# Residual rows ahead of the next stage, no GpSimd drain at two Blocks' ends, and turns between half products in a two-layer hybrid trunk

## What is computed

```python
def odd_mixer(xn, w_in, conv_w, conv_b, w_out):
    gate_b, gate_c, h = jnp.split(xn @ w_in, 3, axis=-1)
    u = gate_c * h
    y = causal_depthwise_conv(u, conv_w) + conv_b
    return (gate_b * y) @ w_out

def expert_block(args):
    xb, e = args
    return (jax.nn.silu(xb @ w_gate[e]) * (xb @ w_up[e])) @ w_down[e]
...
    h = h + mixer(rms_norm(h, mix_norm_g[layer]), ...)
    h = h + hierarchical_moe(rms_norm(h, ffn_norm_g[layer]), ...)
```

## Time and profile before

| | |
|---|---|
| median of 3 runs | 2219.44 us (2216.64 to 2220.0) |
| the profiled execution's own time | 2220.42 us |
| its span in the trace | 2218.7 us |
| PE busy | 1897.2 us (86%) |
| DVE busy | 1228.1 us (55%) |
| ACT busy | 853.2 us (38%) |
| POOL busy | 311.2 us (14%) |
| mean granted clock of TensorE | 0.887 of full speed |

### The profile page before, as it was taken

How to read it: one execution, slowest core, us unless ns; L and a number is a source line. 1 busy time by engine, 2 the same in 40 slices (tenths; PEclk the granted TensorE clock), 3 DMA queues, 4 the chain that set the end, 5 groups by cost and what they waited for, 6 DMA issues and landing times. The chain is left out here.

```text
span 2218.7 us, 25775 instructions
## 1 busy us (share of the span) xinstructions
PE 1897.2 (86%) x9607; PEld 1569.5 (71%) x9608; DVE 1228.1 (55%) x1570; ACT 853.2 (38%) x912; POOL 311.2 (14%) x230
## 2 busy tenths in 40 slices
PE   8999977977589999986999991799999948999970
PEld 7888866767467777874888771588887847888760
DVE  5222115545564553566999883533224557999863
ACT  4110003311223333234888872211112126888850
POOL 0000003000100000112444320000000112443310
PEclk9999985655789999997999995799999978999995
DMA  6321134230200002446999965521124348999927
GB/s 214 129 89 68 48 127 153 71 67 7 77 1 1 1 1 94 162 158 255 363 376 375 374 239 200 180 57 38 47 66 160 133 175 313 383 385 375 364 117 303
DMA packets 146455, 374.22 MB, mean 169 GB/s; under 512 B 40174, under 2 KB 75246, under 8 KB 121614
## 3 DMA queue, kind: packets, MB, share of 16 engines
q1 hardware_dynamic: 117462, 320.82, 39.1%
q0 software_dynamic: 19680, 34.22, 4.1%
q10 hardware_dynamic: 9216, 17.93, 2.1%
HBM read 331.34 MB, written 75.10 MB: 183 GB/s over the span
## 5 line engine op out<-in xcount | busy, mean ns | idle before, releaser
L1037 PE MATMUL ex_ps_h<-even_split 128*128 128x512 f32 x768 | 194.9, 404 | 9.7 <-DVE even_split L1151 9.4
L1037 PE MATMUL ex_ps_h<-odd_split 128*128 128x512 f32 x768 | 195.0, 404 | 7.8 <-DVE odd_split L1151 7.6
L1037 PEld LDWEIGHTS ex_ps_h<-even_split 128*128 128x128 f32 x768 | 141.8, 191 | 49.0 <-DVE even_split L1151 15.2
L1037 PEld LDWEIGHTS ex_ps_h<-odd_split 128*128 128x128 f32 x768 | 141.7, 191 | 47.1 <-DVE odd_split L1151 14.2
L364 PE MATMUL in_ps<-in_w_hi,in_xT_hi 128*128 128x512 f32 (+1 forms) x448 | 169.6, 378 | 1.7 <-DVE in_xT_lo L311 1.7
L364 PE MATMUL in_ps<-in_w_lo,in_xT_hi 128*128 128x512 f32 (+1 forms) x448 | 168.9, 377 | 0.0
L364 PE MATMUL in_ps<-in_w_hi,in_xT_lo 128*128 128x512 f32 (+1 forms) x448 | 168.9, 377 | 0.0
L1418 PE MATMUL conv_ps<-conv_xT_hi,conv_w_hi 128*128 128x512 f32 x384 | 152.0, 396 | 7.5 <-DVE conv_xT_lo L1352 6.6
L1418 PE MATMUL conv_ps<-conv_xT_lo,conv_w_hi 128*128 128x512 f32 x384 | 151.3, 394 | 0.0
L1418 PE MATMUL conv_ps<-conv_xT_hi,conv_w_lo 128*128 128x512 f32 x384 | 151.2, 394 | 0.0
L319 DVE COPY in_stage<-in_ps 128x512 f32<-128x512 f32 (+1 forms) x56 | 36.7, 656 | 197.9 <-PE in_ps L364 197.9
(11 more groups left out here) (329 smaller groups left out, 4175.2 us busy)
## 6 DMA issues: line engine op xcount, KB each, us to landing
all_region<-in_moe_w_gate SPq DMA_DIRECT2D x16, 1024.0 KB, 9.6
all_region<-in_moe_w_up SPq DMA_DIRECT2D x16, 1024.0 KB, 17.8
all_region<-in_moe_w_down SPq DMA_DIRECT2D x16, 1024.0 KB, 16.3
experts_w_gu<-in_moe_w_gate SPq DMA_DIRECT2D x16, 1024.0 KB, 9.9
experts_w_gu<-in_moe_w_up SPq DMA_DIRECT2D x16, 1024.0 KB, 20.2
experts_w_d<-in_moe_w_down SPq DMA_DIRECT2D x16, 1024.0 KB, 15.3
all_region<-in_ev_w_in SPq DMA_DIRECT2D x12, 1024.0 KB, 8.5
proj<-in_stage ACTq DMA_DIRECT2D x48, 256.0 KB, 2.0
```

What stands on the lines that cost most here:

```text
L1037: last = pe.matmul(ps_h[:, u % 2, :], a[:, u % 2, k, :], w[:, k, :], start=(k == 0 and j == 0), stop=(k == KT - 1 and j == 2))
```

## The change

It has three parts.

1. A class `NextRows` holds a view of `region` as 8 tiles and 8 semaphores. SP loads the residual stream's 8 x tiles into it at the end of `experts`, after DVE has reported (`finished`) that it is done. `mix_and_conv` and `finish` use these tiles and load only the ya tiles themselves. In `mix_and_conv` the normed rows and the first column block's raw weights move to the place of `zT_hi`, the raw weights' loads move behind the first four tiles' ya loads, and SP waits for all stores and all norms before it loads column block 1. In `finish` the ya tiles get 8 places, so no load waits for a sum.
2. The Blocks of `project_and_route` and `experts` are opened with `no_gpsimd_drain=True`: POOL executes no DRAIN at their ends. The text calls this "the drain goes"; it holds for four ends, two in each layer.
3. In `mix_and_conv` PE's order changes: five turns come first instead of four, and each of the three others stands between halves (12 matmuls) of the products, where before two of them stood between whole products (24 matmuls) and the last two together behind the third.

Core of the diff:

```diff
@@ -130,8 +130,8 @@
                 self.all[:, gate:gate + qkv].rearrange("p (u n) -> p u n", u=2),
                 self.all[:, gate + qkv:gate + qkv + nq].rearrange("p (u n) -> p u n", u=2))
-    def normed_rows(self):
-        return self.all[:, 0:2 * D].rearrange("p (u n) -> p u n", u=2)
+    def stream_rows(self):
+        return self.all[:].rearrange("p (t n) -> p t n", t=NT)
     def gate_up(self):
         return self.all[:, 0:2 * KT * DE].rearrange("p (j k n) -> p j k n", j=2, k=KT)
@@ -516,7 +516,8 @@
             m.sem(n) for n in ("eps_ready", "bf_ready", "filled", "cleared", "coded", "listed"))
         shifted, exps = m.sem("shifted"), m.sem("exps")
-        with nc.Block() as block:
+
+        with nc.Block(no_gpsimd_drain=True) as block:
             @block.sync
             def _(sp):
                 if rows is not None:
@@ -869,7 +870,18 @@
                 last.then_inc(counted, 1)
-def experts(nc, name, data, lists, slots, most, ident):
+class NextRows:
+
+
+    def __init__(self, m, name, src, region):
+        self.src, self.rows, self.loaded = src, region.stream_rows(), m.sems(name, NT)
+
+    def load(self, sp):
+        for t in range(NT):
+            sp.dma_start(self.rows[:, t, :], self.src[t * P:(t + 1) * P, :]).then_inc(self.loaded[t], 16)
+
+
+def experts(nc, name, data, lists, slots, most, ident, following):
@@ -899,6 +911,7 @@
         FIRST, SECOND, DOWN = range(3)
+        done, finished = m.sb("done", [P, 1]), m.sem("finished")
         zeroed, x_turned = m.sem("zeroed"), m.sems("x_turned", B)
         gathered, idx = lists.gathered, lists.idx
         scattered = m.sems("scattered", U)
@@ -971,6 +985,9 @@
                     with sp.Fori(0, STEPS) as i:
                         round_(w, i)
                 waves(sp, wave, first=1)
+
+                sp.wait_ge(finished, 1)
+                following.load(sp)
             @block.gpsimd
             def _(pool):
@@ -1186,6 +1203,8 @@
                     low(*this, DOWN)
                 dve.memset(data.later_rows, 0.0).then_inc(zeroed, 1)
                 rounds(dve, start, step, lambda last: hidden(*last))
+                dve.drain()
+                dve.memset(done[:], 0.0).then_inc(finished, 1)
 def constants(nc, cst, block):
...
@@ -1214,8 +1233,11 @@
     YA = 4
     with Pool_(nc, name) as m:
         raw = region.conv_weights()
-        xn = region.normed_rows()
-        xin = z_places[0][:].rearrange("p k n -> p (k n)").rearrange("p (t n) -> p t n", t=NT)
+        xin, x_loaded = ahead_rows.rows, ahead_rows.loaded
+        place = z_places[0][:].rearrange("p k n -> p (k n)")
+        xn = place[:, 0:2 * D].rearrange("p (u n) -> p u n", u=2)
+
+        raw_0 = place[:, 2 * D:2 * D + 3 * KT * P].rearrange("p (j k n) -> p j k n", j=3, k=KT)
         ya = z_places[1][:].rearrange("p k n -> p (k n)").rearrange("p (u c n) -> p u c n", u=YA, c=2)
         xT_hi, xT_lo = m.sb("xT_hi", [P, KT, S], F32R), m.sb("xT_lo", [P, KT, S], F32R)
         w_hi = m.sb("w_hi", [P, 3, KT, P], F32R)
...
@@ -1245,7 +1267,6 @@
             @block.sync
             def _(sp):
                 def load_rows(t):
-                    sp.dma_start(xin[:, t, :], src[t * P:(t + 1) * P, :]).then_inc(x_loaded[t], 16)
                     for c in range(2):
                         at = c * S + t * P
                         sp.dma_start(ya[:, t % YA, c, :], slots[at:at + P, :]).then_inc(ya_loaded[t % YA], 16)
@@ -1254,12 +1275,12 @@
                     sp.wait_ge(mixed, t + 1)
                     sp.dma_start(mix_out[t * P:(t + 1) * P, :], xin[:, t, :]).then_inc(stored, 16)
-                for t in range(YA):
+                load_rows(0)
+                sp.dma_start(gains[:], row_of(gain)).then_inc(gain_loaded, 16)
+                for t in range(1, YA):
                     load_rows(t)
-                    if t == 0:
-                        sp.dma_start(gains[:], row_of(gain)).then_inc(gain_loaded, 16)
-                    if t < 3:
-                        sp.dma_start(raw[:, t, :, :], w_k[:, :, PARTS[t] * D:PARTS[t] * D + P]).then_inc(raw_loaded[t], 16)
+                for j in range(3):
+                    sp.dma_start(raw_0[:, j, :, :], w_k[:, :, PARTS[j] * D:PARTS[j] * D + P]).then_inc(raw_loaded[j], 16)
                 for t in range(YA, NT):
                     sp.wait_ge(mixed, t - YA + 1)
@@ -1271,6 +1292,9 @@
                                  allow_slow_non_contiguous=True).then_inc(taps_loaded, 16)
                 for t in range(NT):
                     store_rows(t)
+
+                sp.wait_ge(stored, 16 * NT)
+                sp.wait_ge(normed, NT)
                 with sp.Fori(1, KT) as i:
                     for j in range(3):
                         col = sp.snap(i * P + PARTS[j] * D)
...
@@ -1309,9 +1334,6 @@
                     if more:
                         high(i + 1, 0)
                     act.wait_ge(z_ready, i + 1)
-                    if first:
-
-                        act.wait_ge(stored, 16 * NT)
                     act.activation(zT_hi[:, ds(i, 1), :], z_sb[:].unsqueeze(1), ACT.Copy).then_inc(z_hi, 1)
                 act.wait_ge(eps_ready, 1)
...
@@ -1408,28 +1431,30 @@
                         last = pe.transpose(ps_t[:, k, :], xn[:, t % 2, k * P:(k + 1) * P], cst.ident[:])
                     last.then_inc(turned, 1)
-                def multiply(i, j, half):
-                    if half == 0:
+                def multiply(i, j, half, ks=range(KT)):
+                    if half == 0 and ks[0] == 0:
                         pe.wait_ge(lo_ready[j], i + 1)
                         pe.wait_ge((c_out, u_ready, z_ready)[j], i)
                     at = slice(half * COLS, (half + 1) * COLS)
-                    for k in range(KT):
+                    for k in ks:
                         for q, (w_part, x_part) in enumerate(((w_hi, xT_hi), (w_hi, xT_lo), (w_lo, xT_hi))):
                             last = pe.matmul(ps[:, j, at], w_part[:, j, k, :], x_part[:, k, at],
                                              start=(k == 0 and q == 0), stop=(k == KT - 1 and q == 2))
                     if half == 1:
                         last.then_inc(product[j], 1)
-                for t in range(NT // 2):
+                first, second = range(KT // 2), range(KT // 2, KT)
+                for t in range(5):
                     turn(t)
-                pe.wait_ge(x_low, NT // 2)
-                multiply(0, 0, 0)
-                turn(NT // 2)
-                multiply(0, 1, 0)
-                turn(NT // 2 + 1)
-                multiply(0, 2, 0)
-                turn(NT // 2 + 2)
-                turn(NT // 2 + 3)
+                multiply(0, 0, 0, first)
+                turn(5)
+                multiply(0, 0, 0, second)
+                multiply(0, 1, 0, first)
+                turn(6)
+                multiply(0, 1, 0, second)
+                multiply(0, 2, 0, first)
+                turn(7)
+                multiply(0, 2, 0, second)
                 pe.wait_ge(x_low, NT)
                 for j in range(3):
                     multiply(0, j, 1)
...
@@ -2505,32 +2532,30 @@
                               halves[0][:, gu_n + down_n:gu_n + down_n + 2 * D].rearrange("p (e n) -> p e n", e=2))
                     route(1, "out1", zT_hi, zT_lo, ahead, stream[1], data, lists)
                 moe(1, data, lists)
-            finish(nc, "end", stream[2], slots, gates, out)
-
-
-def finish(nc, name, src, slots, gates, out):
+            finish(nc, "end", following[1], slots, gates, out)
+
+
+def finish(nc, name, ahead_rows, slots, gates, out):
     with Pool_(nc, name) as m:
-        rows = m.sb("rows", [P, NT, D])
-        ya = m.sb("ya", [P, 2, 2, D])
-        loaded, mixed, stored = m.sems("loaded", NT), m.sem("mixed"), m.sem("stored")
+        rows, x_loaded = ahead_rows.rows, ahead_rows.loaded
+        ya = m.sb("ya", [P, NT, 2, D])
+        ya_loaded, mixed, stored = m.sems("ya_loaded", NT), m.sem("mixed"), m.sem("stored")
         with nc.Block() as block:
             @block.sync
             def _(sp):
                 for t in range(NT):
-                    sp.dma_start(rows[:, t, :], src[t * P:(t + 1) * P, :]).then_inc(loaded[t], 16)
-                    if t >= 2:
-                        sp.wait_ge(mixed, t - 1)
                     for c in range(2):
                         at = c * S + t * P
-                        sp.dma_start(ya[:, t % 2, c, :], slots[at:at + P, :]).then_inc(loaded[t], 16)
+                        sp.dma_start(ya[:, t, c, :], slots[at:at + P, :]).then_inc(ya_loaded[t], 16)
             @block.vector
             def _(dve):
                 for t in range(NT):
-                    dve.wait_ge(loaded[t], 48)
+                    dve.wait_ge(x_loaded[t], 16)
+                    dve.wait_ge(ya_loaded[t], 32)
                     for c in range(2):
-                        last = dve.scalar_tensor_tensor(rows[:, t, :], ya[:, t % 2, c, :],
```

(16 more changed lines are left out.)

## The result

The changed kernel takes 2190.65 us (median of 4 runs, 2184.27 to 2197.1) against 2218.11 us before (4 runs, 2216.64 to 2220.0): a ratio of 0.9876, 95% interval 0.9842 to 0.9909. It is 27.5 us faster. The prediction was 2194, with 2182 to 2204 around it.

The account below looks back on a forecast made before the run. PE, busy 86% of the span, was the bound. Routing ends -2.5 and -0.3, layer 0's experts into convolution -9.2, layer 1's into `finish` -13.3: -25.3 from 2220.4 gives 2195.1, predicted 2194 after median correction, range 2182 to 2204.

Parts of the forecast that it names:

- A: Layer 0's routing into its experts: without the DRAIN, PE's first turn starts earlier, -2.5 us.
- C: Layer 1's routing into its experts: DRAIN price moves to L77, only the short barrier is saved, -0.3 us.
- B, DRAIN: Layer 0's experts into the convolution: the removed DRAIN's 5.2 us moves to L77's semaphore clearing, 0 gained.
- B, scatter: End of layer 0's experts: the last scatter lands later beside the early x loads, +3.2 us.
- B, start of the convolution: From SP's first issue to the fourth sum: x tiles already loaded, fewer waits for DMAs, -6.3 us.
- B, PE's order: Convolution, fourth sum to the loop: PE avoids waits for late turns and a second clock fall, -6.1 us.
- D, DRAIN: Layer 1's experts into `finish`: no semaphores are cleared here, so the DRAIN really goes, -5.2 us.
- D, scatter: End of layer 1's experts: the last scatter lands later beside the early x loads, +3.2 us.
- D, `finish`: `finish`: 4.19 MB less to read, -10.2 us, and eight ya places filling gaps, -1.1 us.
- rival 1: Both ends with semaphore clearing: the DRAIN's price goes there too, -5.2 and -3.9 us, total 2185; chance 0.22.
- rival 2: Ends of `experts`: the last scatter isn't delayed by the x loads, -6.4 us, total 2187.5; chance 0.13.
- Rival 4: Convolution's column block 0: PE's clock stays at 1.2 GHz, up to 29 us slower, 2221 to 2224; chance 0.02.

Follow-up runs that it names:

- e3: The kernel before with only POOL's DRAIN removed at the ends of `project_and_route` and `experts`; 2205.41 us, ratio 0.9943.
- e4: The changed kernel with POOL's DRAINs and PE's old order put back, so only the x tiles load early; 2207.17 us, ratio 0.9956 to the kernel before.
- after: The changed kernel's first measurement, with all three parts, against the kernel before; 2190.65 us, ratio 0.9876.
- e2: The kernel before with only PE's new order of turns and half products; 2209.42 us, ratio 0.9962.
- e1: The changed kernel run once more without an edit; 2190.58 us, ratio 0.9875 to the kernel before.
- e5: The changed kernel with SP waiting for the gathers of experts 0 and 1 before loading further weights; 2187.29 us, ratio 0.9861 to the kernel before.
- e8: The changed kernel with a plain POOL DRAIN added in `experts` behind the wait for the last scatters; 2202.28 us, ratio 0.9922 to the kernel before.
- e7: The changed kernel with gathers landing before further weights load and x tiles loaded once their place is free; 2177.05 us, ratio 0.9812 to the kernel before.
- e6: The changed kernel with x tiles loaded as soon as the first expert's buffers are free; 2183.47 us, ratio 0.9824 to the kernel before.

## Why the prediction was right, point by point

The total was right to 3.4 us, but in part by luck. A was taken 3.8 us too favourable and the two scatters 1.9; the DRAIN at B and C 8.2 us too unfavourable and PE's order 1.2. Nothing in the prediction made these misses cancel. The sum on record, -25.3, against what the runs showed of each term:

| term | predicted | shown | by |
|---|---|---|---|
| A | -2.5 | +1.3 | e3 |
| B, DRAIN | 0 | -4.0 | e3 |
| B, scatter | +3.2 | +4.0 | e4 |
| B, start of the convolution | -6.3 | -5.9, -6.5 | after, e4 |
| B, PE's order | -6.1 | -7.3 | e2 |
| C | -0.3 | -4.5 | e3 |
| D, DRAIN | -5.2 | -5.2 | e3 |
| D, scatter | +3.2 | +4.3 | e4 |
| D, `finish` | -11.3 | -11.4, -12.1 | after, e4 |

The terms shown add up to -28.7 to -30.0, by which value is taken where there are two; the kernel gained 27.5 and, in e1, 26.6 us.

**A failed in its sign.** The step was "it was issued one gather ahead, near 1009.1, and lands 4.2 us later"; the sentence behind it, "SP's next loads start earlier too", stood there as a good thing. The gather's 4.2 us were those of a gather beside idle queues, held so by the very DRAIN that goes. Released 1.3 us behind the first gather, SP's weights make it 9.5 us (e3), and with the weights held back it is 4.6 (e5). The bound on record for A, 0, didn't reach to a loss.

**B and C, the DRAIN, failed.** The step was "I take it that the price moves to L77". At B it does not: 0.28 us at most there (e3). At C the first DRAIN of L77 takes 2.58 us (e3), but it lies over POOL's gathers and ends 0.2 us behind them, where the Block's DRAIN ended 4.9 us behind. So the gain of rival 1 came at both places, 4.0 of 5.2 us at B and 4.5 at C, though its sign (L77 still short) held at B alone. At C the forecast's own bound, -4.2 "when gather 0 would bind", is what happened: PE waits for the gather. Rival 1 had a chance of 0.22. The reasoning "a fixed price of the first DRAIN after indirect DMAs" is borne out for a plain DRAIN placed behind the wait at layer 1 (e8, 5.2 us; 6.7 at layer 0), and not for the DRAINs that are part of the clearing.

**The scatter beside the x loads was right in kind and 0.8 and 1.1 us too small.** It lands in 7.6 and 7.5 us (e4) where 7 and 6.3 were taken; 7 less the 3.6 of a scatter alone is also 3.4, not 3.2. Of rival 2 (no delay) nothing came true. The Trainium skill, page "DMA: Bandwidth & Descriptors", section "Queues, rings and completion order", has an engine go round its queue rows packet by packet; the equal shares that the prediction made of that, +1.3 us, are not borne out by +4.0 and +4.3. Of the two readings the trace's own 8.9 us was the nearer. The 0.5 MB of that estimate were too much as well: in the kernel before POOL's queue moves 0.19 MB for the last scatter at D.

**The convolution's start and `finish` were right.** DVE takes over as the bound once its second sum has started, as worked out, though that sum came 10.3 us behind SP's first issue and not 9.4. `finish` is 11.4 us shorter, 31.06 us from the first issue to the last sum, where 31 was written down. How that divides between the x tiles' transfer (10.2 on record) and the eight places for ya tiles (1.1) no run shows, since none has one without the other.

**PE's order was right, 1.2 us too small.** PE has no wait between turn 4 and the last one, and the clock does not fall again. It also rises in the first group of 12 matmuls, whose starts go from 0.43 to 0.23 us apart at 1405.6 (0.72 of full speed over 1401.0 to 1409.3), where the sum had all 12 at 1.2 GHz. The last wait is 1.28 us, where the prediction took 0.9. Rival 4 (the clock stays low) is out.

The three parts alone make -7.8, -11.8 and -10.0, together -29.6; the changed kernel has -26.6 on the same chip. Each of these gains is known to 3 to 4 us only, so the 3 us between are not shown to be anything. In the traces they lie in no term of the table but in the experts' stretches, which take 329.5 to 330.3 us in the changed kernel's two and 327.4 to 329.0 in those of e2 to e4; in e7 they take 327.0 and 326.6.

## What to carry to other kernels

A drain or a barrier that looks like pure cost may also be what keeps transfers apart: before it goes, ask which DMAs it holds back, and let the short transfer that someone waits for land before the bulk is released (e5, 3.7 us at A). A prefetch should start as soon as its place is free, not when its stage is over, because at the stage's end it can meet the last small write that everybody waits for (e6, some 4 us at each end). Where POOL itself has waited for its indirect DMAs, ask whether a further plain DRAIN of POOL is needed: here it took 5.2 to 6.7 us (before, e8).

## What the runs showed of the hardware that was not expected

- A plain DRAIN of POOL behind indirect DMAs that have landed takes 5182 to 5203 ns in five of the six places at the ends of `experts` in before, e4 and e8, and 6742 ns in the sixth. With no such DRAIN ahead of it, the first DRAIN in the clearing of semaphores takes 283 ns at most there (after, e1, e3), and about 2590 ns where POOL's two gathers are still being issued (C, the same runs).
- The stages ahead of the change, the same in all these kernels, do not take the same time: the split of layer 0 starts between 998.4 us (e4) and 1007.0 us (e6). These 8.5 us are more than most of the terms that were looked for, so the total of one profiled execution can't show such a term; a stretch counted from an event near it can.
